# One diffusion step on one core: token gathers for several experts at once, and the combine's place

## The reference

```python
def moe_swiglu(h, w_router, we_gate, we_up, we_down):
    x = h.reshape(b * s, d)
    top_v, top_i = lax.top_k((x @ w_router).astype(jnp.float32), 2)
    gates = ...            # softmax of the two, spread over the 8 experts
    for e in range(8):
        y = y + gates[:, e:e + 1] * swiglu(x, we_gate[e], we_up[e], we_down[e])
```

## Time and profile before

| | |
|---|---|
| median of 3 runs | 1453.07 us (1451.85 to 1454.02) |
| profiled execution | 1458.25 us, its span 1456.4 us |
| PE busy | 1397.2 us (96%) |
| DVE, ACT busy | 367.4 us (25%), 258.1 us (18%) |
| weights and all else read from HBM | 463.33 MB |
| gate/up L1768, down L1783 | 582.1 us, 291.3 us |
| gather L1698, combine L1717 | 32.9 us, 14.8 + 13.1 us |

### The profile page before, as it was taken

The page is one execution under the profiler, slowest core; times in us unless marked ns, Lnnn a source line. Parts: engine busy times, 40 slices in busy tenths (PEclk is TensorE's granted clock), DMA queues, the critical chain, the costliest instruction groups (busy, mean ns, idle before and its releaser), DMA issues.

```text
span 1456.4 us, 28545 instructions
## 1 busy us (share of the span) xinstructions
PE 1397.2 (96%) x12744; PEld 733.7 (50%) x12744; DVE 367.4 (25%) x608; ACT 258.1 (18%) x409; POOL 28.3 (2%) x60
## 2 busy tenths in 40 slices
PE   6798899999997999999999999999999999999996
PEld 3766699999774963333333333333333333333332
DVE  1433554554624321001101100201111111200213
ACT  1523554443514210000000000000000000000001
POOL 0030000000030000000000000000000000000000
PEclk8899899999999989999999999999999999999998
DMA  9766978654754489999999999999999999999970
GB/s 348 253 221 224 314 264 291 201 195 158 265 180 166 165 353 369 420 364 367 421 370 364 421 379 363 407 385 372 395 387 382 387 421 342 384 420 364 373 329 30
DMA packets 129226, 466.54 MB, mean 320 GB/s; under 512 B 9770, under 2 KB 52564, under 8 KB 98388
## 3 DMA queue, kind: packets, MB, share of 16 engines
q1 hardware_dynamic: 126800, 462.72, 82.9%
q10 hardware_dynamic: 2308, 2.02, 0.4%
HBM read 463.33 MB, written 1.38 MB: 319 GB/s over the span
## 4 chain that ended last, share of the span: by engine, by line
PE 94%; DVE 3%; ACT 2%; issue 1%; DMA 0%; ACTq 0%; DVEq 0%
PE ps L1768 40%; PE ps L1783 20%; PE ps L1438 5%; PE ps L1439 5%; PE ps L1440 5%; PE ps L1399 2%; PE ps L1698 2%; PE ps L1449 2%; PE ps L1613 1%; PE ps L1612 1%; PE ps L1614 1%; PE ps L1371 1%; PE ps L1717 1%; PE ps L1409 1%; PE ps L1529 1%
## 5 line engine op out<-in xcount | busy, mean ns | idle before, releaser
L1768 PE MATMUL ps<-ering,xg 128*32 128x512 f32 (+1 forms) x6144 | 582.1, 539 | 0.7 <-ACT xg L865 0.7
L1768 PEld LDWEIGHTS ps<-ering,xg 128*32 128x32 f32 x6144 | 199.2, 110 | 375.9 <-issue 373.9
L1783 PE MATMUL ps<-ering,eT 128*32 128x512 f32 x2688 | 291.3, 592 | 0.0
L1438 PE MATMUL ps<-hx,high 128*128 128x256 f32 x640 | 181.2, 283 | 17.7 <-DVE low L945 13.2
L1783 PEld LDWEIGHTS ps<-ering,eT 128*32 128x32 f32 x2688 | 86.6, 110 | 195.8 <-issue 195.1
L1440 PE MATMUL ps<-hx,low 128*128 128x256 f32 x640 | 179.6, 281 | 0.0
L1439 PE MATMUL ps<-hx,high 128*128 128x256 f32 x640 | 179.5, 280 | 0.0
L945 DVE TENSOR_TENSOR low<-ring,high 128x1024 fp32r<-128x1024 f32 x102 | 121.9, 1223 | 88.6 <-ACT high L685 88.6
L1438 PEld LDWEIGHTS ps<-hx,high 128*128 128x128 f32 x640 | 122.5, 191 | 22.4 <-DVE low L945 14.6
L1440 PEld LDWEIGHTS ps<-hx,low 128*128 128x128 f32 x640 | 122.7, 192 | 0.0
L1439 PEld LDWEIGHTS ps<-hx,high 128*128 128x128 f32 x640 | 122.4, 191 | 0.0
(11 more groups left out here) (207 smaller groups left out, 845.3 us busy)
## 6 DMA issues: line engine op xcount, KB each, us to landing
ering<-in_moe_w_down SPq DMA_DIRECT2D x112, 1024.0 KB, 10.1
ering<-in_moe_w_gate SPq DMA_DIRECT2D x64, 1024.0 KB, 7.7
ering<-in_moe_w_up SPq DMA_DIRECT2D x64, 1024.0 KB, 9.8
ring<-in_w_ada SPq DMA_DIRECT2D x48, 1024.0 KB, 7.3
ering<-in_moe_w_gate SPq DMA_DIRECT2D x64, 768.0 KB, 6.8
ering<-in_moe_w_up SPq DMA_DIRECT2D x64, 768.0 KB, 8.3
ring<-in_ffn_w_gate SPq DMA_DIRECT2D x11, 1024.0 KB, 5.5
ring<-in_ffn_w_up SPq DMA_DIRECT2D x11, 1024.0 KB, 7.8
```

Source lines behind the costliest of these rows:

```text
L1438: mm(out, hi[:, k, :], xh, start=n == 0, stop=False)
L1768: last = mm(ps[32 * c:32 * c + 32, bank, 0:width].rearrange("p (n r) -> p n r", r=64), xg[:, kk, 32 * g:32 * g + 32], w[t][:, c, :, :], st ...
L1783: last = mm(ps[32 * group:32 * group + 32, bank, :], eT[s][:, g, 2 * i + odd, :], w[:, odd, 512 * half:512 * (half + 1)], start=(s, i) == ...
```

## The change

In the first round only expert 0 is gathered by itself, as before. The gathers of experts 1, 2, 3 stand together in expert 0's downs and those of 4 to 7 in expert 3's; each group in two turns of 4 chunks, the first behind the fifth down item of step 0, the second behind the eighth. A matmul there takes the columns of three or four experts at once (288 or 384), and computes in fp32r: h2 is split into h2h and h2l, so there are two one-pass matmuls for one in fp32. Banks 0 to 3 hold a turn. `xg` keeps four experts. P is held as fp32r (`P1`), and read as fp32 where it was before.

The two stops of `combine` (and of `turn_places` in expert 0) go from chunk 3 of step 0 and chunk 1 of step 1 to chunks 2 and 4 of step 0; VectorE adds all four quarters before step 0's products. To make room, `eT` of step 0 shares memory with Yh and Yl, `eT` of step 1 lies where small tiles of the earlier layers were, and `fin` where `mrow` was. Experts 1 to 6 of the first round are written out on ScalarE and VectorE too. Further rounds keep a gather for each expert, with two fp32r matmuls for one.

```diff
+TOGETHER = 4
+GROUPS = {0: (1, 2, 3), 3: (4, 5, 6, 7)}
+def gathers_before(e, rnd):
+    if rnd:
+        return 1 + 2 * len(GROUPS) + NE * (rnd - 1) + e + 1
+    return 1 + 2 * sum(e >= group[0] for group in GROUPS.values())
...
-        P = sb("P", 128, NE, 2, CAP)
+        h2l = nc.alloc_sbuf_tensor_at("h2l", [128, 2, D], f32r, offset=h2_at)
+        h2h = sb("h2h", 128, 2, D, dt=f32r)
+        P1 = sb("P1", 128, NE, 2, CAP, dt=f32r)
+        P = P1[:, :, :, :].bitcast(f32)
...
 # ScalarE (VectorE alike, with m in (2, 3))
+            def take_group(group):
+                for turn in range(2):
+                    act.wait_ge(gat_done, gathers_before(group[0], 0) - 1 + turn)
+                    for m in (0, 1):
+                        last = A(xg[:, 4 * turn + m, group[0] % TOGETHER:group[-1] % TOGETHER + 1, :],
+                                 ps[:, GATHER_BANK + m, 0:len(group) * CAP].rearrange("p (e t) -> p e t", t=CAP), ACT.Copy)
+                    last.then_inc(xg_first_ready, 1)
...
+                if rnd == 0:
+                    act.wait_ge(h2_ready, 1)
+                    for b in range(2):
+                        A(h2h[:, b, :], h2[:, b, :], ACT.Copy).then_inc(h2h_ready, 1)
...
 # VectorE
+                if rnd == 0:
+                    for b in range(2):
+                        dve.wait_ge(h2h_ready, b + 1)
+                        V.tensor_tensor(h2l[:, b, :], h2[:, b, :], h2h[:, b, :], ALU.subtract).then_inc(h2l_ready, 1)
+                    dve.wait_ge(stored, 32 * DEPTH)
...
-                        if begins:
-                            take_PT(rnd, s)
-                        else:
-                            add_up(e, k, (2 * s, 2 * s + 1))
+                        add_up(e, k, range(4))
...
 # TensorE
+            def gather_group(group, turn):
+                if turn:
+                    n = gathers_before(group[0], 0) - 1
+                    pe.wait_ge(xg_first_ready, n)
+                    pe.wait_ge(xg_last_ready, n)
+                else:
+                    pe.wait_ge(P_ready, group[-1] + 1)
+                    pe.wait_ge(h2h_ready, 2)
+                    pe.wait_ge(h2l_ready, 2)
+                for m in range(4):
+                    out = ps[:, GATHER_BANK + m, 0:len(group) * CAP].rearrange("p (e t) -> p e t", t=CAP)
+                    for b in range(2):
+                        for part in (h2h, h2l):
+                            k = 4 * turn + m
+                            last = mm(out, part[:, b, k * 128:(k + 1) * 128], P1[:, group[0]:group[-1] + 1, b, :],
+                                      start=b == 0 and part is h2h, stop=b == 1 and part is h2l)
+                last.then_inc(gat_done, 1)
...
-                            if kk == (3, 1)[s]:
+                            if s == 0 and kk in (2, 4):
+                                turn = (2, 4).index(kk)
                                 if begins:
-                                    turn_places(s)
+                                    turn_places(turn)
                                 else:
-                                    combine(k, (2 * s, 2 * s + 1))
+                                    combine(k, (2 * turn, 2 * turn + 1))
...
                         for i in range(E_WIDTH[s] // 64):
                             down(s, i)
-                        if s == 0 and not ends:
-                            pe.wait_ge(eh_ready, k * NSTEP * SG + NSTEP * SG)
-                            gather(e + 1)
+                            if s == 0 and i == 4:
+                                pe.wait_ge(eh_ready, k * NSTEP * SG + NSTEP * SG)
+                                if rnd == 0 and e in GROUPS:
+                                    gather_group(GROUPS[e], 0)
+                        if s == 0:
+                            if rnd:
+                                if not ends:
+                                    gather(e + 1, rnd)
+                            elif e in GROUPS:
+                                gather_group(GROUPS[e], 1)
```

More of the change, by code:

```diff
@@ L886, in expert @@
                         take_Y(k)
+                    for turn in range(2) if begins else ():
+                        act.wait_ge(PT_done, 2 * rnd + turn + 1)
+                        A(PT[0:CAP, 4 * turn:4 * turn + 2, :, :], ps[0:CAP, PLACES_BANKS[0], :].rearrange("p (e b t) -> p e b t", e=2, b=2), ACT.Copy).then_inc(PT_first_ready, 1)
                     for s, width in enumerate(E_WIDTH):
-                        if begins:
-                            act.wait_ge(PT_done, 2 * rnd + s + 1)
-                            A(PT[0:CAP, 4 * s + 1:4 * s + 3, :, :], ps[0:CAP, PLACES_BANKS[0], :].rearrange("p (e b t) -> p e b t", e=2, b=2), ACT.Copy).then_inc(PT_first_ready, 1)
                         for g in range(SG):
@@ L893, in expert @@
                             A(sg[:, g, 0:width], ps[:, GATE_BANKS[g], 0:width], ACT.Silu).then_inc(esg_ready, 1)
-                    if not ends:
-                        take_xg(k + 2)
-                expert(0, begins=True)
-                with act.Fori(1, NE - 1) as e:
-                    expert(e)
+                    if rnd:
+                        if not ends:
+                            take_xg(gathers_before(e + 1, rnd))
+                    elif e in GROUPS:
+                        take_group(GROUPS[e])
+                expert(0, begins=True)
+                if rnd == 0:
+                    for e in range(1, NE - 1):
+                        expert(e)
+                else:
+                    with act.Fori(1, NE - 1) as e:
+                        expert(e)
                 expert(NE - 1, ends=True)
@@ L1229, in take_xg, with take_group @@
                 dve.wait_ge(gat_done, n)
-                V.tensor_copy(xg[:, 4:8, :], ps[:, GATHER_BANK + 1, 0:4 * CAP].rearrange("p (k t) -> p k t", k=4)).then_inc(xg_last_ready, 1)
+                V.tensor_copy(xg[:, 4:8, 0, :], ps[:, GATHER_BANK + 1, 0:4 * CAP].rearrange("p (k t) -> p k t", k=4)).then_inc(xg_last_ready, 1)
+            def take_group(group):
+                for turn in range(2):
+                    dve.wait_ge(gat_done, gathers_before(group[0], 0) - 1 + turn)
+                    for m in (2, 3):
+                        last = V.tensor_copy(xg[:, 4 * turn + m, group[0] % TOGETHER:group[-1] % TOGETHER + 1, :],
+                                             ps[:, GATHER_BANK + m, 0:len(group) * CAP].rearrange("p (e t) -> p e t", t=CAP))
+                    last.then_inc(xg_last_ready, 1)
             def add_Y(e, n, even=Y_even_ready, added=Y_ready, high_half=Yh_ready, low_half=Yl_ready, now=now_ready):
-                places = PT[0:CAP, e, :, :] if isinstance(e, int) else PT[0:CAP, bass.ds(e, 1), :, :].rearrange("p o b t -> p (o b) t")
+                places = PT[0:CAP, e - 1, :, :] if isinstance(e, int) else PT[0:CAP, bass.ds(e - 1, 1), :, :].rearrange("p o b t -> p (o b) t")
                 V.tensor_copy(PT_now[0:CAP, :, :], places).then_inc(now, 1)
@@ L1301, in expert @@
                                         hm[:, turn % 2, 0:width].rearrange("p (n r o) -> p n o r", r=32, o=2)).then_inc(eT_ready, 1)
-                    if not ends:
-                        take_xg(k + 2)
-                expert(0, begins=True)
-                with dve.Fori(1, NE - 1) as e:
-                    expert(e)
+                    if rnd:
+                        if not ends:
+                            take_xg(gathers_before(e + 1, rnd))
+                    elif e in GROUPS:
+                        take_group(GROUPS[e])
+                expert(0, begins=True)
+                if rnd == 0:
+                    for e in range(1, NE - 1):
+                        expert(e)
+                else:
+                    with dve.Fori(1, NE - 1) as e:
+                        expert(e)
                 expert(NE - 1, ends=True)
@@ L1690, in _, with gather @@
             last.then_inc(rank_done, 1)
-            def gather(e):
+            def gather(e, rnd):
+                parts = (h2h, h2l) if rnd else (h2,)
+                places = P1 if rnd else P
                 for m in range(KD):
                     for b in range(2):
-                        rhs = P[:, e, b, :] if isinstance(e, int) else P[:, bass.ds(e, 1), b, :].rearrange("p o t -> p (o t)")
-                        last = mm(ps[:, GATHER_BANK + m // 4, (m % 4) * CAP:(m % 4 + 1) * CAP], h2[:, b, m * 128:(m + 1) * 128], rhs, start=b == 0, stop=b == 1)
+                        rhs = places[:, e, b, :] if isinstance(e, int) else places[:, bass.ds(e, 1), b, :].rearrange("p o t -> p (o t)")
+                        for part in parts:
+                            last = mm(ps[:, GATHER_BANK + m // 4, (m % 4) * CAP:(m % 4 + 1) * CAP], part[:, b, m * 128:(m + 1) * 128], rhs,
+                                      start=b == 0 and part is parts[0], stop=b == 1 and part is parts[-1])
+                last.then_inc(gat_done, 1)
[4 more added lines that the diff above has]
```

(9 more changed lines are left out.)

47 lines of the change are left out of this document (28 added, 19 removed).

## The result

| | before | changed |
|---|---|---|
| median of the runs shown together | 1452.46 us (1447.31 to 1454.02, 4 runs) | 1437.24 us (1435.23 to 1438.09, 4 runs) |
| ratio | | 0.988, 95% interval 0.9855 to 0.9905 |
| profiled execution | 1458.25 us | 1438.09 us |
| first gate product to last down instruction, start to start | 912.47 us | 896.59 us |
| PE busy | 1397.2 us | 1374.9 us |

What follows compares the result with a forecast made beforehand. TensorE's own work was taken to bound the kernel. Old gathers removed, 27.1 us, less new gathers, 10.1, save 17.0 us, everything else costed at nothing: from a median of 1453.07 to 1436.0 us, range 1433.0 to 1441.5.

Steps and rivals of the forecast that it cites:

- What bounds the kernel: In the experts, TensorE's issued work sets the time; weight transfers, at DMA share 0.96 to 0.97, do not.
- What goes: Seven gathers leave the middle of the experts: 3.88 us each, 27.2 us, taken as 27.1.
- What comes: Two grouped gathers, 288 and 384 columns, at 0.127 and 0.170 us a matmul, four entries of 0.14: 10.1 us.
- The second turn's wait: Before a group's second turn, TensorE waits for copies of the first: 6 us of cover; uncovered, 1.2 us twice.
- the moved wait for eh_ready: Wait for the last expert product, moved from behind the eighth down item to behind the fifth: costs nothing.
- the combine's place: Combine's two stops moved to behind slices 2 and 4 of step 0: covers 11.9 and 10.3 us, cost 0.
- the unrolled code: Experts written out on ScalarE and VectorE: claimed to add no work.
- the split of h2: Passes on ScalarE and VectorE after the first xg, 4.9 us: costs nothing; if exposed, 4.9 us once.
- A: In the new gathers weight loads add to streaming: 21.7 us, saving only 4.9, 1448 us; chance 0.04.
- B: Transfers set the pace once TensorE is faster: an expert stays about 114.6 us, time 1453 us; chance 0.03.
- C: New gather products are not one-pass: 36.1 us + 0.6, 9.6 us slower, 1462.7 us; chance 0.03.
- D: Straight-line code on ScalarE and VectorE fetched late, 3.9 us in each of six experts: 6.4 us slower, 1459.5; chance 0.03.

Runs made afterwards that it cites:

- e9: Changed kernel without any gather but expert 0's, experts 1 to 7 computing with expert 0's tokens, all weights loaded: stretch 885.30 us.
- e10: Changed kernel with the third group of 32 slots left out of the gate/up products of chunks 1 to 6, all weights loaded: stretch 825.94 us.
- e4: Changed kernel with P1 laid out so that a group's columns lie in one run without gaps: stretch 896.49 us.
- e7: Changed kernel with a group's first turn behind the eighth down item, directly before the second turn: stretch 898.59 us.
- e3: Kernel before with experts 1 to 6 written out on ScalarE and VectorE and the combine's new place, old gathers kept: stretch 912.56 us, ratio 0.9984.
- e8: Changed kernel with the combine's two stops behind chunks 0 and 1 of step 0 in place of 2 and 4: stretch 896.58 us.
- e1: Changed kernel with seven groups of one expert each, one-pass gathers of 96 columns: stretch 914.27 us, ratio 1.0003 against the kernel before.

## Why the prediction was right, point by point

**What bounds the kernel.** Right. TensorE's own work made the stretch: taking 11.3 us more of it away took 11.3 us off (e9). The DMA share of 0.97 was no sign of a bound; lead and rate told it before, and in e10 the transfers kept up with a stretch 71 us shorter.

**What goes.** 27.1 us. e9 is the changed kernel without any later gather, so 912.47 - 885.30 = 27.17 us is what the seven old ones cost. Right to 0.1 us.

**What comes.** This term was too small: 10.1 us forecast, 896.59 - 885.30 = 11.3 measured, inside the bounds of 8.0 and 11.9. Of the 1.2 us, 0.4 is the spacing: 32 x (0.134 + 0.176) = 9.9 us, not 9.5. About 0.1 of that are the gaps between the runs of 96 columns, which were costed at nothing (e4). The rest is in the choice of row. The projections' 0.113 us at 256 columns was taken as a price per column, but it lies next to the floor of 0.112 that one, 96 and 192 columns show too, so it says little of the columns. The combine, used for the upper bound, was priced at 0.285 us by its whole stop, with the way in and out; its inner starts are some 0.235 us apart, and a line to that from the projections gives 0.128 and 0.174, 9.7 us, nearer but still low.

The other 0.8 us is the entries. Four of 0.14 us were counted, the loss in the downs behind a gather; but a turn's own first and last distances are longer too (0.24 and 0.22 us with 288 columns): 2.35 us are 16 x 0.134 and 0.21 more, so an entry costs 0.34 us (0.21 + 0.13). In the old gather that part was hidden in the 3.74 us, spread over 32 instructions.

**Waits and covers.** The second turn's wait, the moved wait for eh_ready, the combine's place, the unrolled code and the split of h2 were costed at nothing. The first is shown by its opposite (e7, about 1 us each when uncovered), the moved wait by the list of waits, which has none in the stretch but the 0.7 us, the place and the code by e3 and e8. The split was not tried alone; its last part ends at 525.65 us on VectorE, and its first reader starts at 609.95.

**Sum and range.** 27.2 - 11.3 = 15.9 us in the stretch against 17.0; the whole miss is the term of the new gathers, and no second error stands against it. The medians, 1437.24 and 1438.94 us, lie within 1433.0 to 1441.5. They are 1.2 and 2.9 us above the forecast; since medians of the kernel before differ by as much (1452.46 and 1455.26 us), the stretch is the better test.

**The rivals.** A fell: loads of 0.19 us lie beside matmuls 0.134 us apart. But what spoke for it, the floor, was real, and it makes one pass alone worth nothing. B fell with the wait list, e9 and e10; the limit of about 358 GB/s that the Trainium skill gives for one core ("DMA: Bandwidth & Descriptors", section "Specifications") does not hold in this case, where the core moved 419 GB/s for 700 us (e10). C fell in its condition and not in its price: each product of a group is one instruction, and even in fp32 a column costs 2 x 0.84 ns = 1.68 ns, the price that was worked out. D fell with e3.

## What to carry to other kernels

A matmul with fresh full-array weights had a floor in every run here: about 0.112 us at full granted clock, from one column up to 192 and nearly the same at 256. Below it neither fewer passes nor fewer columns help, only fewer matmuls, so widen first, then cut passes: here the second alone won nothing (and 1.8 us went on its extra entries), the first alone won 7.8, both 15.9. Count an entry for each block of matmuls as well, 0.34 us here. And when a row is used as a price per column, check that it is not standing on such a floor; two widths above it give the slope.

## What the runs showed that was not expected

The part ahead of the experts took 514.9 to 528.1 us in thirteen profiled executions of kernels nearly alike up to there, and it goes with the granted clock. The clock's records add up to 34 us at the lower level ahead of the stretch in e1, the shortest (mean granted clock 0.97 up to 530 us). In the other twelve (mean 0.94 to 0.95) they add up to 58 us where that part ended at 522.5 to 523.8, 61 where it ended at 523.4 to 525.6, 65 at 527.3, and 68 at 526.7 and 528.0. That scatter is nearly as large as the whole effect, while the stretch with TensorE always busy, at clock 1.00, was 896.586 and 896.585 us in the two profiles of the changed kernel. What makes the clock fall in one execution and not in the next stays open.

The price of one-pass columns is not quite one clock each: 0.112 us at 96 and 192 columns, 0.113 at 256 in the projections, 0.134 at 288, 0.176 at 384, while the two passes of an fp32 instruction take 0.243 us for 288 and 0.323 for 384, that is 0.1215 and 0.1615 a pass. One-pass matmuls are 9 to 10% slower per pass than those. The gaps in the columns explain little of it (e4); no run tells what the cause is.
